# Small products between the rows of the next in-projection unit, a two-row start of two units in the ramps, and a first gate that leaves ahead of a weight split

## The chip, the cores and the metric

The kernel runs on one core of one Trainium2 chip. The metric is device time in microseconds (us) of one execution of the whole program. TensorE (PE) multiplies, VectorE (DVE), ScalarE (ACT) and GpSimd (POOL) do the element work, and SyncE (SP) issues most DMAs.

## The reference, cut to what matters

One layer of a hybrid decoder on 512 prompt tokens and 32 sample tokens (544 columns), model width 1024:

```python
x = x + 0.5*rmsnorm(swiglu(rmsnorm(x)))      # FFN1, inner width 2816
x = x + rmsnorm(mix(rmsnorm(x)))             # in-projection 1024 -> 2432, four mixers, out-projection
x = x + 0.5*rmsnorm(swiglu(rmsnorm(x)))      # FFN2, inner width 2816
```

In the mixer, group C (RWKV-7) takes seven of the 19 in-projection tiles, and needs three low-rank products and a normalised key before its scan:

```python
w_log = -softplus(-(w0 + tanh(wl) @ w2)) - 0.5       # low-rank product 1, 32 rows
a     = sigmoid(a0 + al @ a2)                        # low-rank product 2, 32 rows
g     = sigmoid(gl) @ g2                             # low-rank product 3, 64 rows
kk    = k*k_k ;  kk = kk * rsqrt(max(sum(kk*kk), 1e-24))   # sum over each head of 64
```

## The kernel before, in words

**Units.** Everything is held transposed: features on the 128 partitions, the 544 tokens as columns in two halves of 272. A unit is one 128-wide slice of a weight matrix times all 1024 input features: 8 rows (one row is a block of 128 input features, index `j`), each row three products (high part times high, high times low, low times high, which together give float32 accuracy), each in two halves, so 48 matmuls at line 315 (`product`).

**What a unit needs.** SP loads its weights into one of two raw buffers. ACT rounds them to the high part (`split_hi`, line 293), DVE subtracts to get the low part (`split_lo`, line 298), and PE waits for that in `split_ready`. Four split slots are used in turn. A unit's result lies in a pair of PSUM banks until DVE takes it out.

**Every engine works through its own list in order**, written out by hand; semaphores join the lists. A step that waits holds back everything behind it on its engine.

**The ramps** (`ramp_pe`) join FFN1 to the mixer and the mixer to FFN2. The input `x` of the next part is only coming into being: DVE and ACT make its rows one after the other (`rows_dve`: update at line 507, add at 512, low part at 522; ACT's high part at 517), first for token half 0 and then for half 1. PE takes row `j` for units 0, 1 and 2 as soon as it is there, and unit 3 later; between them it makes the sums of squares (line 375, which wait for DVE's lines 487 and 490) and spreads the roots (line 384).

**The in-projection** (`mixer_pe`, `mixer_act`, `mixer_dve`). Units 0 to 3 are the ramp; units 4 to 18 follow one by one. Before unit m PE waits for `split_ready(m)` and for `in_out`: DVE has taken out unit m-2 (for m of 6 and more; its `leave`, line 2220). DVE's list is, for each m: `split_lo(m)`, `leave(m-2)`, then the token shift of that tile (`shifted`, lines 2171 to 2175, for the seven tiles of group C) and what belongs to m: the scans of the decay (m = 7), three operations for each of two halves of `kp` and `bo` (m = 8), the keys' normalisation. ACT's list is, for each m from 6: `split_hi(m)`, and then what belongs to m. The parts of it around the change stand in this order:

```python
split_hi(5); tanh, sigmoid -> lo2                                   # m = 3
wait lora 1, 2: sigmoid -> bt (two halves, line 2078)               # m = 5
split_hi(6); wait lora 3, 4: sigmoid -> bh (line 2082)              # m = 6
split_hi(7); wait lora 5, 6: copy -> gg (2086); 2 squares -> kt (2089)  # m = 7
split_hi(8); wait kk_max: root (line 2092)                          # m = 8
split_hi(9); exponentials of the decay, half 0 (2097 to 2103)       # m = 9
split_hi(10); exponentials, half 1                                  # m = 10
```

The small products of group C stand on PE in blocks between units: low-rank product 1, 2 and 3 (`lora`, line 1953) after units 4, 5 and 6; the keys' sums (line 1962) after unit 7; the spread of their roots (line 2054) after unit 8; the bonus' sums (line 1974) after unit 10. These products are plain float32, and one of them shows as two matmul instructions. ACT reads the two halves of `lora` with one step each, and the next low-rank product waits for that step (`lora_out`), since it writes to the same banks. POOL starts the pooling mixer's additions (lines 1368 to 1374) once DVE has taken out unit 8.

**The start of an FFN.** Units are gate and up in turn: unit 0 is the gate of inner tile 0, unit 1 its up, units 2 and 3 those of tile 1. DVE multiplies the gate by the norm (line 1105, semaphore `gate`), ACT applies silu (line 1095), DVE multiplies by the up (line 1109, `h_mul`) and splits the result (`hidden_dve`). In the loop over the other tiles (`ffn_pe`, group 0) PE waits, before each unit, for the split, and for the hidden tile that frees its banks (`h_mul`). In FFN2 ACT's list is `split_hi(4)`, silu; DVE's is `split_lo(4)`, then the whole of `hidden_dve` for tile 0, then the rows of `qb` (lines 970 and 971).

Of the kernel before, what the change touches and what calls it, by code (L numbers as in the profile page):

```python
# [30 lines left out]
P = 128  # L31
# [83 lines left out]
def program(nc, a, o):  # L115

    with ExitStack() as ctx:
# [138 lines left out]
        def pair(n):  # L256
            return ps[:, 2 * n:2 * n + 2, 0:H]
# [312 lines left out]
        def ramp_pe(pe, n, u):  # L570

            def come(h, j):
                pe.wait_ge(S("n_xl"), row(n, h, j) + 1)

            pe.wait_ge(S("n_rb"), mark(n, 0, 0) + 1)
            for j in range(KD):
                come(0, j)
                for s in range(3):
                    if j == 0:
                        split_ready(pe, u, 0, s)  # L580
                    product(pe, pair(s), s, (j,), xh, xl, opens=j == 0, closes=j == KD - 1, parts=(0,))
                if j == 2:
                    half_sums_pe(pe, n, 1, 0)
                if j == 3:
                    half_sums_pe(pe, n, 1, 1)
                    half_spread_pe(pe, n, 1, 0)
                if j == 4:
                    pe.wait_ge(S("n_rb"), mark(n, 0, 1) + 1)
                    split_ready(pe, u, 0, 3)
                    product(pe, pair(3), 3, range(5), xh, xl, closes=False, parts=(0,))  # L590
                if j > 4:
                    product(pe, pair(3), 3, (j,), xh, xl, opens=False, closes=j == KD - 1, parts=(0,))
                if j == 5:
                    half_spread_pe(pe, n, 1, 1)
            pe.wait_ge(S("n_rb"), mark(n, 1, 1) + 1)
            for j in range(KD - 2):
                come(1, j)
                for s in range(4):
                    product(pe, pair(s), s, (j,), xh, xl, opens=j == 0, closes=False, parts=(1,))
            for s in range(4):  # L600
                product(pe, pair(s), s, (KD - 2, KD - 1), xh, xl, None if s else lambda j: come(1, j), opens=False, parts=(1,)
                        ).then_inc(S("unit_done"), 1)
# [431 lines left out]
        def ffn_pe(pe, q, u0, n):  # L1034
            u, dn = u0, 0

            def input_ready(j):
                pe.wait_ge(S("n_xl"), j + 1)

            for s in range(0 if q else 4):  # L1040
                split_ready(pe, u, 0, s)
                if s == 3:
                    pe.wait_ge(S("n_rb"), 1)
                if s == 2:
                    product(pe, pair(s), s, range(KD // 2), xh, xl, closes=False)
                    spread_root_pe(pe)
                    product(pe, pair(s), s, range(KD // 2, KD), xh, xl, opens=False).then_inc(S("unit_done"), 1)
                    continue
                product(pe, pair(s), s, range(KD), xh, xl, input_ready if s == 0 else None).then_inc(S("unit_done"), 1)
                if s == 1:  # L1050
                    pe.wait_ge(S("in_con"), 48)
                    sums_pe(pe)
            for g, (f0, nf) in enumerate(GROUPS):
                if g:
                    with pe.Fori(0, nf // 2) as i:
                        for s in range(2):
                            fast_pe(pe, q, g, i, s, dn)
                else:
                    with pe.Fori(1, nf // 2) as i:
                        for s in range(4):  # L1060
                            split_ready(pe, u, i, s)
                            pe.wait_ge(S("h_mul"), i * 2 + (FT * q + f0 + s // 2 + 1))
                            pe.wait_ge(S("d_out"), 20 * q + dn + s + 1)
                            product(pe, pair(s), s, range(KD), xh, xl).then_inc(S("unit_done"), 1)
                    u += 2 * nf

                def hidden_ready(j):
                    pe.wait_ge(S("h_lo"), FT * q + f0 + j + 1 + 2)

                def down_free(d):  # L1070
                    pe.wait_ge(S("d_out"), 20 * q + dn + d + 1)

                if g == 2:
                    for s in range(4):
                        split_ready(pe, u, 0, s)
                        pe.wait_ge(S("h_mul"), FT * q + f0 + nf + 2 - (s < 2))
                        down_free(s)
                        product(pe, pair(s), s, range(nf), hh, hl, hidden_ready if s == 0 else None
                                ).then_inc(S("unit_done"), 1)
                    last_units_pe(pe, 4 * q + 1, u, 0, range(nf), hh, hl, down_free)  # L1080
                    continue
                with pe.Fori(0, 2) as i:
                    for s in range(4):
                        split_ready(pe, u, i, s)
                        pe.wait_ge(S("h_mul"), FT * q + f0 + nf + 2 - (s < 2))
                        pe.wait_ge(S("d_out"), i * 4 + (20 * q + dn + s + 1))
                        product(pe, pair(s), s, range(nf), hh, hl, hidden_ready if s == 0 else None
                                ).then_inc(S("unit_done"), 1)
                u += KD
                dn += KD  # L1090
# [4 lines left out]
            act.activation(silu[:, s % 2], silu[:, s % 2], ACT.Silu).then_inc(S("silu"), 1)  # L1095

        def hidden_dve(dve, q, u, i, f0, s):

            unit_done(dve, u, i, 2 * s)
            dve.wait_ge(S("h_mul"), i * 2 + (FT * q + f0 + s + 1))  # L1100
# [2 lines left out]
            else:  # L1103
                dve.wait_ge(S("n_rb"), 1)
            dve.tensor_tensor(halves(silu[:, s % 2]), pair(2 * (s % 2)), halves(rb[:]), MUL).then_inc(S("gate"), 1)
            unit_done(dve, u, i, 2 * s + 1)
            dve.wait_ge(S("silu"), i * 2 + (FT * q + f0 + s + 1))
            dve.wait_ge(S("h_lo"), i * 2 + (FT * q + f0 + s + 1))
# [34 lines left out]
        def ffn_act(act, q, u0, n):  # L1143
# [4 lines left out]
            for g, (f0, nf) in enumerate(GROUPS):  # L1148
# [12 lines left out]
                for s in range(0 if q == 0 else 4, 4):  # L1161
                    if s > 1:
                        split_hi(act, u, 0, s, KD)
                    if s == 3:
                        root_act(act)
                        rb_act(act)
                if q:
                    split_hi(act, u + 4, 0, 0, KD)
                silu_act(act, q, 0, f0, 0)
                for s in range(1 if q else 0, 2 * nf - 4):  # L1170
# [13 lines left out]
        def ffn_dve(dve, q, u0, n):  # L1184
# [4 lines left out]
            for g, (f0, nf) in enumerate(GROUPS):  # L1189
# [7 lines left out]
                for s in range(0 if q == 0 else 4, 4):  # L1197
                    if s > 1:
                        split_lo(dve, u, 0, s, KD)
                    if s == 3:  # L1200
                        stats_dve(dve)
                if q:
                    split_lo(dve, u + 4, 0, 0, KD)
                hidden_dve(dve, q, u, 0, f0, 0)
                if q:
                    rows_mul_dve(dve, q, 0, False)
                for s in range(1 if q else 0, 2 * nf - 4):
# [728 lines left out]
        def mixer_pe(pe):  # L1936
            A, B = pair(2), pair(3)

            ramp_pe(pe, 1, MIX0)
            for m in range(4, NIN):  # L1940
                split_ready(pe, MIX0, 0, m)
                in_out(pe, {4: 0, 5: 1}.get(m, m - 2))
                product(pe, pair(in_pair(m)), m % 4, range(KD), xh, xl).then_inc(S("unit_done"), 2 if m == NIN - 1 else 1)
                if m in (4, 5, 6):

                    rows = (slice(0, 32), slice(32, 64), slice(64, P))[m - 4]
                    in_out(pe, 3)
                    for p in range(2):
                        pe.wait_ge(S("lo2"), 1)
                        if m > 4:  # L1950
                            pe.wait_ge(S("lora_out"), 2 * (m - 4) - 1 + p)
                        for n in range(2):
                            last = pe.matmul((A, B)[p][:, n], lora_w[rows, P * p:P * p + P],
                                             (lo if m == 5 else lo2)[rows, n * H:n * H + H], start=True, stop=True)
                        last.then_inc(S("lora"), 1)
                if m == 7:
                    pe.wait_ge(S("lora_out"), 5)
                    pe.wait_ge(S("kk_sq"), 2)
                    for p in range(2):
                        for t in range(5):  # L1960
                            c = (p * 5 + t) * 2
                            last = pe.matmul(ps[:, 4, c:c + 2], kt[:, p, tok(t)], hsel, start=True, stop=True)
                    last.then_inc(S("kk_sum"), 1)
                if m == 8:
                    pe.wait_ge(S("kk_rec"), 1)
                    pe.wait_ge(S("lora_out"), 6)
                    for p in range(2):
# [89 lines left out]
        def mixer_act(act):  # L2057
            for m in range(3, NIN + 2):
# [24 lines left out]
                if m == 7:  # L2083
# [3 lines left out]
                    for p in range(2):  # L2087
                        act.wait_ge(S("kkraw"), p + 1)
                        act.activation(kt[:, p], ar[:, p, 0], ACT.Square).then_inc(S("kk_sq"), 1)
                if m == 8:  # L2090
                    act.wait_ge(S("kk_max"), 1)
                    act.activation(st[:, 1, 0:20], st[:, 0, 0:20], ACT.Sqrt).then_inc(S("kk_root"), 1)
                if m in (9, 10):
# [40 lines left out]
        def mixer_dve(dve):  # L2134
# [89 lines left out]
            for m in range(2, NIN + 2):  # L2224
# [51 lines left out]
                if m == 8:  # L2276
                    for p in range(2):
# [2 lines left out]
                        do(dve.tensor_scalar(tmp2[:, p], bh[:, p], par_("ka", p), onemka[:, p:p + 1], MUL, ADD))  # L2280
                        do(dve.tensor_tensor(kp[:, p], kp[:, p], tmp2[:, p], MUL))
                        dve.scalar_tensor_tensor(bo[:, p], ar[:, p, 1], par_("rk", p), kp[:, p], MUL, MUL).then_inc(S("rk"), 1)
                    dve.wait_ge(S("kk_sum"), 1)
                    dve.tensor_scalar(st[:, 0, 0:20], ps[:, 4, 0:20], 1e-24, None, ALU.max).then_inc(S("kk_max"), 1)
                    dve.wait_ge(S("kk_root"), 1)
# [241 lines left out]
```

## Time and profile before

| | |
|---|---|
| median of 3 runs | 1118.23 us (1114.58 to 1122.45) |
| the profiled execution | 1122.75 us, its span 1120.9 us |
| mean granted clock of PE | 0.961 |
| PE busy (weight loads) | 1073.6 us, 96% (1050.4 us, 94%) |
| DVE, ACT, POOL busy | 798.0, 461.6, 275.6 us |
| DMA | 92.04 MB, mean 82 GB/s |

Busy time of PE counts a matmul from start to its modelled end, so that matmuls overlap. "PEclk" is the granted clock: 1.00 is 2.4 GHz, 0.50 is 1.2 GHz. A timeline row gives start, duration, the instruction and, in brackets, how long the engine had been idle and what ended that. A row marked x2 or more merges instructions that follow each other. The stages in the profiled execution: FFN1 up to 391 us, the first ramp 391 to 427, the in-projection's other units 427 to 536, the rest of the mixer to 720, the second ramp 720 to 755, FFN2 to the end.

### The profile page before, as it was taken

The page shows a single profiled execution, that of the slowest core. Times are in us where ns is not written, and L with a number is a line of the kernel's source. Part 1 is how long each engine was busy: PE and PEld are TensorE (multiplying, and loading weights), DVE is VectorE, ACT ScalarE, POOL GpSimd, SP SyncE. Part 2 cuts the span into 40 slices and gives each one's busy share as a digit, 9 for nine tenths or more (in the row PEclk, how much of TensorE's full clock was granted, in tenths as well). Part 3 has the DMA queues.
Part 4 walks back from the last instruction along what each step waited for, and adds up shares of the span by engine and source line. Part 5 has one row for each costly group of instructions (what it writes and reads, how often), then busy time and mean ns, then how long its engine had stood idle before and what let it go on. Part 6 is the DMA issues. An engine that isn't in the chain of part 4 may idle for free. (4 is left out here: it accounts for less than half of the span.)

```text
span 1120.9 us, 23284 instructions
## 1 busy us (share of the span) xinstructions
PE 1073.6 (96%) x9138; PEld 1050.4 (94%) x9138; DVE 798.0 (71%) x1224; ACT 461.6 (41%) x776; POOL 275.6 (25%) x217
## 2 busy tenths in 40 slices
PE   6999999999999989999799999999999999999995
PEld 6999999999999989999677789899999999999995
DVE  5667689536986886888769627967577984399746
ACT  6423455414654433522134433433235552256520
POOL 0220656034540000120223000004125531255201
PEclk9999999999999989999779989989999999999998
DMA  6322233322324121232601002203132324223212
GB/s 215 97 90 91 84 112 108 102 91 76 112 75 132 40 71 57 79 68 87 68 2 40 2 1 80 74 23 110 58 130 75 112 75 150 76 75 112 91 60 81
DMA packets 35400, 92.04 MB, mean 82 GB/s; under 512 B 10368, under 2 KB 12928, under 8 KB 35328
## 3 DMA queue, kind: packets, MB, share of 16 engines
q1 hardware_dynamic: 34320, 88.78, 25.7%
q10 hardware_dynamic: 1008, 2.27, 0.6%
q8 instruction: 49, 0.80, 0.3%
q14 instruction: 23, 0.19, 0.1%
HBM read 87.76 MB, written 3.28 MB: 81 GB/s over the span
## 5 line engine op out<-in xcount | busy, mean ns | idle before, releaser
L315 PE MATMUL ps<-xh,wh 128*128 128x272 f32 x816 | 195.3, 302 | 18.8 <-DVE xl L499 8.6
L824 PE MATMUL ps<-seven,wh 128*128 128x272 f32 x1024 | 195.1, 287 | 0.0
L315 PE MATMUL ps<-xl,wh 128*128 128x272 f32 x816 | 191.0, 297 | 0.0
L315 PE MATMUL ps<-xh,wl 128*128 128x272 f32 x816 | 190.8, 297 | 0.0
L298 DVE TENSOR_TENSOR wl<-raw,wh 128x1024 fp32r<-128x1024 f32 (+1 forms) x99 | 118.7, 1201 | 81.1 <-ACT wh L293 80.7
L315 PEld LDWEIGHTS ps<-xh,wh 128*128 128x128 f32 x816 | 140.8, 197 | 21.9 <-DVE wl L298 12.1
L824 PEld LDWEIGHTS ps<-seven,wh 128*128 128x128 f32 x1024 | 159.8, 188 | 0.0
L315 PE MATMUL ps<-hh,wh 128*128 128x272 f32 x704 | 156.2, 288 | 0.0
L315 PE MATMUL ps<-hh,wl 128*128 128x272 f32 x704 | 155.4, 288 | 0.0
L315 PE MATMUL ps<-hl,wh 128*128 128x272 f32 x704 | 155.1, 287 | 0.0
L293 ACT ACTIVATE wh<-raw 128x1024 fp32r<-128x1024 f32 (+1 forms) x99 | 100.0, 1018 | 126.8 <-PE ps L315 58.7
L824 PE MATMUL ps<-seven,wl 128*128 128x272 f32 x512 | 146.7, 286 | 0.0
L315 PEld LDWEIGHTS ps<-xl,wh 128*128 128x128 f32 x816 | 141.4, 198 | 0.0
L315 PEld LDWEIGHTS ps<-xh,wl 128*128 128x128 f32 x816 | 140.5, 198 | 0.0
L802 DVE TENSOR_TENSOR wl<-sums,wh 128x1024 fp32r<-128x1024 f32 x64 | 93.6, 1463 | 42.2 <-ACT wh L797 42.0
L315 PEld LDWEIGHTS ps<-hl,wh 128*128 128x128 f32 x704 | 114.1, 188 | 0.0
L315 PEld LDWEIGHTS ps<-hh,wl 128*128 128x128 f32 x704 | 113.8, 188 | 0.0
L315 PEld LDWEIGHTS ps<-hh,wh 128*128 128x128 f32 x704 | 113.7, 188 | 0.0
L780 POOL TENSOR_TENSOR sums<-raw 128x512 f32<-128x512 f32 x32 | 42.6, 1331 | 282.5 <-DMA raw<-in_w_gu 246.8
L824 PE MATMUL ps<-xl,wh 128*128 128x272 f32 x384 | 111.1, 289 | 0.0
L824 PE MATMUL ps<-xh,wh 128*128 128x272 f32 x384 | 110.4, 287 | 0.0
L824 PE MATMUL ps<-xh,wl 128*128 128x272 f32 x384 | 109.9, 286 | 0.0
(348 smaller groups left out, 1910.4 us busy)
## 6 DMA issues: line engine op xcount, KB each, us to landing
raw<-in_w_gu SPq DMA_DIRECT2D x88, 512.0 KB, 3.7
raw<-in_w_d SPq DMA_DIRECT2D x32, 512.0 KB, 3.6
raw<-in_w_in SPq DMA_DIRECT2D x19, 512.0 KB, 3.6
raw<-in_w_d SPq DMA_DIRECT2D x16, 384.0 KB, 3.0
raw<-in_w_out SPq DMA_DIRECT2D x8, 512.0 KB, 3.6
out_y<-x SPq DMA_DIRECT2D x16, 136.0 KB, 1.8
x<-in_x ACTq DMA_DIRECT2D x4, 272.0 KB, 5.5
x<-in_x SPq DMA_DIRECT2D x4, 272.0 KB, 6.6
```

Of the source, the lines that this page charges most:

```text
L293: act.activation(wh[:, s % 4, 0:k, :], src[:, s % RAW, 0:k, :], ACT.Copy).then_inc(S("w_hi"), 1 + skip)
L298: dve.tensor_tensor(wl[:, s % 4, 0:k, :], src[:, s % RAW, 0:k, :], wh[:, s % 4, 0:k, :].bitcast(F32), SUB).then_inc(S("w_lo"), 1 + skip)
L315: last = pe.matmul(out[:, n], left[:, s, j], right[:, j, n * H:n * H + H], start=first and opens and j == order[0], stop=final and closes ...
L780: pool.tensor_tensor(sum_(0), up[:, 0:4], up[:, 4:8], ADD).then_inc(S("f_sum"), 1)
L802: dve.tensor_tensor(left_to(wl, k), left_of(s, k), left_to(wh, k).bitcast(F32), SUB).then_inc(S("f_lo"), 1)
L824: last = pe.matmul(out, left[:, j], right[:, j], start=m in (0, 1, 3) and j == 0 and left is hi and right is high, stop=j == 3 and left is ...
```

## The change

In the ramps, units 0 and 1 take rows 0 and 1 first, and unit 2 opens at row 1 with both rows. In the in-projection, low-rank product k (0, 1, 2) is issued inside unit 5+k, a quarter of it before each of the rows 1, 3, 5 and 7; the keys' sums are issued inside unit 8, a fifth before each of the rows 3 to 7; the spread stands after unit 9. ACT's root and DVE's three steps for it move from m = 8 to m = 9. In the FFNs' group 0, a gate unit waits for `gate` of the tile two before it (its banks have been read) and no longer for `h_mul`; in FFN2, DVE takes out the first gate before `split_lo(4)`, and ACT issues a one-column silu ahead of `split_hi(4)`. ACT's order of splits and low-rank steps stays.

```diff
@@ ramp_pe
-                for s in range(3):
-                    if j == 0:
+                for s in range(2 if j == 0 else 3):
+                    if j == s // 2:
                         split_ready(pe, u, 0, s)
-                    product(pe, pair(s), s, (j,), xh, xl, opens=j == 0, closes=j == KD - 1, parts=(0,))
+                    product(pe, pair(s), s, range(2) if j + s == 3 and j == 1 else (j,), xh, xl, opens=j == s // 2, closes=j == KD - 1,
+                            parts=(0,))
@@ ffn_pe, group 0
-                            pe.wait_ge(S("h_mul"), i * 2 + (FT * q + f0 + s // 2 + 1))
+                            if s % 2:
+                                pe.wait_ge(S("h_mul"), i * 2 + (FT * q + f0 + s // 2 + 1))
+                            else:
+                                pe.wait_ge(S("gate"), i * 2 + (FT * q + f0 + s // 2 - 1))
@@ ffn_act
                 if q:
+                    act.activation(st2[:, 1, 7:8], ones[:, 0:1], ACT.Silu)
                     split_hi(act, u + 4, 0, 0, KD)
@@ ffn_dve   (hidden_dve is cut into first_gate_dve and second_dve)
+                first_gate_dve(dve, q, u, 0, f0, 0)
                 if q:
                     split_lo(dve, u + 4, 0, 0, KD)
-                hidden_dve(dve, q, u, 0, f0, 0)
+                second_dve(dve, q, u, 0, f0, 0)
@@ mixer_pe
+            def lora_pe(k, p, n):
+                rows = (slice(0, 32), slice(32, 64), slice(64, P))[k]
+                if p + n == 0:
+                    in_out(pe, 3)
+                    pe.wait_ge(S("lo2"), 1)
+                if k and n == 0:
+                    pe.wait_ge(S("lora_out"), 2 * k - 1 + p)
+                last = pe.matmul((A, B)[p][:, n], lora_w[rows, P * p:P * p + P], (lo if k == 1 else lo2)[rows, n * H:n * H + H],
+                                 start=True, stop=True)
+                if n:
+                    last.then_inc(S("lora"), 1)
+            def keys_sum_pe(t):
...
+            def between(m):
+                def before(j):
+                    if m in (5, 6, 7) and j % 2:
+                        lora_pe(m - 5, j // 4, j // 2 % 2)
+                    if m == 8 and j > 2:
+                        keys_sum_pe(j - 3)
+                return before
...
-                product(pe, pair(in_pair(m)), m % 4, range(KD), xh, xl).then_inc(S("unit_done"), 2 if m == NIN - 1 else 1)
-                if m in (4, 5, 6):
...
-                if m == 7:
...
-                if m == 8:
+                product(pe, pair(in_pair(m)), m % 4, range(KD), xh, xl, between(m)).then_inc(S("unit_done"), 2 if m == NIN - 1 else 1)
+                if m == 9:
                     pe.wait_ge(S("kk_rec"), 1)
@@ mixer_act
-                if m == 8:
+                if m == 9:
                     act.wait_ge(S("kk_max"), 1)
@@ mixer_dve
+                if m == 9:
                     dve.wait_ge(S("kk_sum"), 1)
```

## Rows read from the trace of the kernel before

**Rows 1.** The chain that ended last, FFN2: start us, us, what.
```profile
757.08 85.66 PE ps L315 x672
926.74 47.79 PE ps L315 x384
```

**Rows 2.** Timeline of PE around units 4 to 11 of the in-projection.
```profile
433.27 0.41 PE L315 MATMUL ps<-xh,wl 128*128 128x272 f32 x2
434.45 2.07 PE L1953 MATMUL ps<-lor,lora_w 32*128 32x272 f32 x8 [0.77 <-ACT lor L2074]
436.45 0.77 PE L315 MATMUL ps<-xh,wh 128*128 128x272 f32 x2
...
444.19 2.10 PE L1953 MATMUL ps<-lor,lora_w 32*128 32x272 f32 x8
...
460.59 2.29 PE L1962 MATMUL ps<-con,kt 128*128 128x2 f32 x20
...
470.46 2.17 PE L2054 MATMUL ps<-con,st 128*64 128x128 f32 x40
...
484.70 2.00 PE L1974 MATMUL ps<-bo,con 128*128 128x272 f32 x8
```

**Rows 3.** Timeline of ACT in the in-projection.
```profile
436.55 0.72 ACT L2078 ACTIVATE bt<-ps,par 128x544 f32<-128x544 f32 x1 [0.20 <-PE ps L1953]
437.17 1.05 ACT L293 ACTIVATE wh<-raw 128x1024 fp32r<-128x1024 f32 x1
...
455.09 1.20 ACT L2089 ACTIVATE kt<-ar 128x544 f32<-128x544 f32 x2
...
466.68 1.28 ACT L2097 ACT_TABLE_LOAD   x1
467.98 0.21 ACT L2097 ACTIVATE pend<-ll 128x8 f32<-128x8 f32 x1
```

**Rows 4.** Timeline of DVE in the in-projection.
```profile
438.25 1.23 DVE L298 TENSOR_TENSOR wl<-raw,wh 128x1024 fp32r<-128x1024 f32 x1
439.39 0.85 DVE L2220 TENSOR_TENSOR pc<-ps,rb 128x272 f32<-128x272 f32 x3
...
457.26 1.22 DVE L298 TENSOR_TENSOR wl<-raw,wh 128x1024 fp32r<-128x1024 f32 x1
...
465.30 0.17 DVE L2284 TENSOR_SCALAR st<-ps 128x20 f32<-128x20 f32 x1
...
474.33 2.38 DVE L2293 SCALAR_TENSOR_TENSOR bhkh<-ar,bhkh 128x544 f32<-128x544 f32 x1
...
479.63 2.21 DVE L298 TENSOR_TENSOR wl<-raw,wh 128x1024 fp32r<-128x1024 f32 x1
```

**Rows 5.** Three stretches: busy of PE, PEld, DVE, ACT, POOL, PEclk, DMA share, GB/s.
```profile
433.50:441.00 7.50, 6.74 (x34) 5.96 (x33) 7.36 (x18) 3.17 (x5) 0.00 (x0) 0.77 0.06 11
462.00:470.00 8.00, 8.00 (x54) 8.00 (x55) 5.63 (x11) 4.44 (x9) 0.00 (x0) 0.79 0.12 29
757.00:761.00 4.00, 3.92 (x19) 3.92 (x20) 3.93 (x7) 0.16 (x1) 1.26 (x1) 0.57 0.23 90
```

**Rows 6.** The first ramp: PE opens unit 2; then DVE's low part of row 2.
```profile
394.54 0.39 PE L315 MATMUL ps<-xh,wh 128*128 128x272 f32 x1 [2.06 <-DVE wl L298]
395.70 0.50 DVE L522 SCALAR_TENSOR_TENSOR xl<-x,par,xh 128x272 fp32r<-128x272 f32 x1
```

**Rows 7.** The start of FFN2: timelines of ACT, DVE and PE.
```profile
752.57 1.06 ACT L293 ACTIVATE wh<-raw 128x1024 fp32r<-128x1024 f32 x1 [3.44 <-PE ps L315]
753.65 1.28 ACT L1095 ACT_TABLE_LOAD   x1
753.66 1.23 DVE L298 TENSOR_TENSOR wl<-raw,wh 128x1024 fp32r<-128x1024 f32 x1 [4.00 <-ACT wh L293]
754.81 0.72 DVE L1105 TENSOR_TENSOR silu<-ps,rb 128x544 f32<-128x544 f32 x1
757.08 0.59 PE L315 MATMUL ps<-xh,wh 128*128 128x272 f32 x2 [2.35 <-DVE h L1109]
```

More of the change, by code:

```diff
@@ L1097, in hidden_dve, with first_gate_dve @@
         def hidden_dve(dve, q, u, i, f0, s):
+            first_gate_dve(dve, q, u, i, f0, s)
+            second_dve(dve, q, u, i, f0, s)
+        def first_gate_dve(dve, q, u, i, f0, s):
             unit_done(dve, u, i, 2 * s)
@@ L1105, in hidden_dve, with second_dve @@
             dve.tensor_tensor(halves(silu[:, s % 2]), pair(2 * (s % 2)), halves(rb[:]), MUL).then_inc(S("gate"), 1)
+        def second_dve(dve, q, u, i, f0, s):
             unit_done(dve, u, i, 2 * s + 1)
@@ L1937, in mixer_pe @@
             A, B = pair(2), pair(3)
+            def lora_pe(k, p, n):
[10 more added lines that the diff above has]
+            def keys_sum_pe(t):
+                if t == 0:
+                    pe.wait_ge(S("lora_out"), 5)
+                    pe.wait_ge(S("kk_sq"), 2)
+                for p in range(2):
+                    c = (p * 5 + t) * 2
+                    last = pe.matmul(ps[:, 4, c:c + 2], kt[:, p, tok(t)], hsel, start=True, stop=True)
+                if t == 4:
+                    last.then_inc(S("kk_sum"), 1)
+            def between(m):
[5 more added lines that the diff above has]
+                return before
             ramp_pe(pe, 1, MIX0)
@@ L1942, in mixer_pe @@
                 in_out(pe, {4: 0, 5: 1}.get(m, m - 2))
-                product(pe, pair(in_pair(m)), m % 4, range(KD), xh, xl).then_inc(S("unit_done"), 2 if m == NIN - 1 else 1)
-                if m in (4, 5, 6):
[L1946 to L1955, printed above, removed]
-                if m == 7:
[L1957 to L1963, printed above, removed]
-                if m == 8:
+                product(pe, pair(in_pair(m)), m % 4, range(KD), xh, xl, between(m)).then_inc(S("unit_done"), 2 if m == NIN - 1 else 1)
+                if m == 9:
                     pe.wait_ge(S("kk_rec"), 1)
```

## The prediction, made before the changed kernel was run

> **What bounds the kernel now.** I read the chain of waits first. In FFN2 it is PE's own stream of full-size products [rows 1]: one matmul per 47.79/384 = 0.1245 us, so a unit of 48 takes 6.0 us and a row of one unit 0.75 us. PE is the bound there, and what is won or lost ahead of FFN2 reaches the end whole. I then read PE's timeline through the stretches that the change touches, and looked for its gaps and for the small products. In the in-projection PE hardly stops: one gap of 0.77 us before the first low-rank block, and then blocks of 2.1, 2.3, 2.2 and 2.0 us [rows 2]. So an order that hides these blocks' waits can win little, and one that opens a new gap loses it. Last I read ACT and DVE between the same times, to see what stands between a low-rank product and the next unit's weights: ACT's `bt` step ends, and `split_hi(6)` starts at once [rows 3]. That is the order of ACT's list, not of its data.
>
> The granted clock is the second thing to see. The 7.5 us after the gap of 0.77 ran at 0.77, the 8 us after the keys' block at 0.79, and the 4 us after FFN2's opening gap of 2.35 at 0.57 [rows 5, 7]: each time a spell at 1.2 GHz instead of 2.4, at the price of 7.5 x 0.23, 8 x 0.21 and 4 x 0.43, that is 1.7 us of PE's time each.
>
> **Low-rank products inside units.** The matmuls are the same and cost the same 2.1 us a block wherever they stand [rows 2]. What changes is when their last part comes. Unit 5 can start at 433.5, right behind unit 4 [rows 2], 2.9 us before its 436.45, and saves the gap and the spell after it. It then holds the first low-rank product, 6.0 + 2.1 = 8.1 us, the last quarter in front of row 7. ACT can't finish `bt` before that quarter is out, and `split_hi(6)` is behind `bt`. From the start of the second `bt` step to `split_hi(6)` is 437.17 - 436.55 = 0.6 us, from there to `split_lo(6)` 1.1 us, from there to the taking out of unit 4, which unit 6 also needs, 1.1 us, and that takes 0.85 us [rows 3, 4]: 3.7 us with hand-overs. Row 7 covers 0.75 us of it. PE stands still for 3.0 us before unit 6, where it had the low-rank block of 2.1 us to work on before. Unit 7 is behind `bh`, inside unit 6, in the same way: 3.0 us. Unit 8 is behind `gg` and ACT's two squares, 1.1 us more [rows 3]: 4.1 us. (The next low-rank product waits for `lora_out` of the last, long given.)
>
> Starts, at full clock: unit 5 at 433.5, unit 6 at 433.5 + 8.1 + 3.0 = 444.6, unit 7 at 455.7, unit 8 at 455.7 + 8.1 + 4.1 = 467.9, unit 9 at 467.9 + 6.0 + 2.3 = 476.2, and behind it the spread, so unit 10 at 476.2 + 6.0 + 2.2 = 484.4. Before, unit 10 started 6.0 ahead of the bonus block, at 478.7 [rows 2]. That is **+5.7 us**, with the two spells of before (in units 5 and 8) on the old side and none on the new.
>
> What could be late next: DVE's own work from `split_lo(8)` to the keys' maximum is 465.30 - 457.26 = 8.0 us [rows 4], and with `split_lo(9)` and a taking out it now runs from 2.0 us before unit 8 to 8.0 us after its start; unit 8 ends 8.3 after it. I cost it at nothing; without that cover it would be tenths. The keys' steps moved to m = 9 end before unit 9's sixth us, and DVE's and ACT's parts of 0.2 to 0.3 us lie beside unit 9: nothing. Behind the root on ACT come a table load, half a set of exponentials and `split_hi(10)`; they have unit 9 and the spread, 8.2 us, as cover: nothing. The row shows the load at 1.28 us with the next step 0.02 us behind it [rows 3]. By the Trainium skill (ScalarE: Activation LUTs, What ACT_TABLE_LOAD costs) a switch costs a drain of about 1.38 us more; by that ACT would be later by as much at each load, and unit 10 by a few tenths. I take the row. After the spread DVE now starts on the keys only about when unit 10 does. From 474.33 to 479.63 and `split_lo(11)` of 2.21, both long because POOL's additions run beside them [rows 4], and a taking out, make some 9 us from the spread's middle; unit 10 and the bonus block are 8.0. POOL's work is released by the same unit, so it runs beside the same DVE steps as before. I take nothing, and 1 us as the upper bound. SP's loads of weights follow `split_lo` two units earlier, and move with it.
>
> **The clock.** Gaps of 3.0, 3.0 and 4.1 us are each longer than the 0.77, 2.06 and 2.35 us after which PE's clock fell or PE waited [rows 2, 6, 7]. I take one spell after each: 3 x 1.7 = **+5.1 us**. Below, nothing; above, two spells for each, 10.2 us. The keys' sums, spread over five rows, should save their spell, which the +5.7 has already counted.
>
> **Ramps.** In the first ramp PE waited 2.06 us for unit 2's split and restarted at 394.54. Row 1 for units 0 and 1, 0.75 us, now goes into that gap, and unit 2's two rows end at about 395.3. But row 2's low part leaves DVE at 395.70 + 0.50 = 396.2 [rows 6], and DVE waits for nothing that moved. So PE stops there instead: **0**, with 0.6 us as the bound on either side (what a shifted gap could do to the clock). The second ramp has the same order: 0.
>
> **The start of FFN2.** PE waited 2.35 us for DVE's line 1109 [rows 7]. Now the first gate leaves while ACT makes `split_hi(4)`; DVE's split still ends at 753.66 + 1.23 = 754.9, and that is what unit 4 waits for, since its banks are free once the gate (0.72 us, from 752.5) is out. It starts at about 754.95 instead of 757.08: 2.1 us, and the spell behind the gap, 1.7 us, goes too, since 0.4 us of gap is under all that were followed by one. **-3.8 us.** ACT's new one-column silu and the table load of 1.28 us fall in its idle 3.44 us before 752.57 [rows 7]. Unit 5's split follows 1.5 us earlier, ahead of its need. Bounds: 0 and -3.8. In the other loops DVE has finished a hidden tile before the split that PE also waits for: nothing.
>
> **Sum.** 5.7 + 5.1 + 0 - 3.8 = +7.0 us on the profiled execution, 1122.75 + 7.0 = 1129.8. That execution is 4.5 us above the median of the runs, so I put the forecast at 1118.23 + 7.0 = **1125.2 us**. About 1%, 11.2 us, is what a measurement can tell from no change.
>
> **Rivals.**
> - *Slower by over 1%.* In units 6, 7 and 8 each gap costs two spells at 1.2 GHz. It decides once a gap is so long that the clock does not come back after one spell; for it speaks that the gaps are longer than any seen before in these stretches, against it that 2.35 us cost just one [rows 5, 7]. 5.7 + 10.2 - 3.8 = +12.1: 1130.3 us. Chance 0.22.
> - *The gaps come, the clock holds.* 5.7 - 3.8 = +1.9: 1120.1 us. Against it speak the rows of the three spells. Chance 0.08. The Trainium skill (TensorE: Matmul & The Clock Gate, HAM oscillation) lets the clock fall back only over long waits between bursts; by that this rival would be the likely one, and the trace here does not agree, with its spell after 2.35 us.
> - *The splits are not held up*, because ACT comes to them earlier than I read from its list. Then PE saves the gap and the spells of units 5 and 8, 0.8 + 3.4, and FFN2's 3.8: 1110.2 us. Against it: the split starts as `bt` ends [rows 3]. Chance 0.07.
> - *FFN2's gain does not come*, something else holding unit 4: +10.8, 1129.0 us. Chance 0.06.
> - The forecast, one spell for each gap: chance 0.57, its own range 1121 to 1130.
>
> **Range and chances.** From between the third rival's time and the second's up to past the first's, with the 4 us by which runs scatter: 1115 to 1133. Slower by over 1% (above 1129.4): the first rival's most, and the upper tail of the forecast and of the fourth, 0.22. Faster by over 1% (below 1107): a part of the third, 0.03. Within: 0.75.
>
> **What would show it.** Right: PE's timeline has gaps near 3 us in front of units 6 and 7 and near 4 in front of unit 8, each ended by DVE (split or taking out), with ACT's `split_hi` right behind `bt`, `bh` and the squares; PEclk below 1 after each; no block of low-rank products between units; unit 4 of FFN2 starting behind DVE's line 298 with under 1 us of gap. Wrong: these gaps missing or under 1 us, ACT's splits ahead of its low-rank steps, or a total under 1115 us.

## The result: slower by 2.0%, where +0.6% was forecast

| | forecast | measured |
|---|---|---|
| median | 1125.2 us (1115 to 1133) | 1142.47 us (1137.88 to 1143.73, 4 runs) |
| the kernel before, beside it | | 1120.34 us (1114.58 to 1125.5, 4 runs) |
| ratio | 1.006 | 1.0198 [1.0154, 1.0241] |
| profiled execution, its span | 1129.8 us | 1142.94 us, 1141.2 us |
| mean granted clock | | 0.955 (before 0.961) |

The direction is right and the size is not: the time lies 9 us above the range. The first rival, slower by over 1% through a second spell at 1.2 GHz behind each gap, had 0.22; its own time, 1130.3 us, is too low as well. The experiments below were timed in three sets, each on another chip, with the kernel before beside them (its medians: 1123.01, 1122.21 and 1121.03 us); so results of different sets are compared by their ratios to it, with their 95% intervals, and the ratio is not the quotient of the two medians.

The page of the changed kernel shows PE's busy time and the granted clock in 40 slices of 28.5 us. Slices 16 and 17 (428 to 485 us) hold the changed units of the in-projection, and their digits are 8 and 7.

```profile
span 1141.2 us, 23289 instructions
PE 1084.3 (95%) x9138; PEld 1054.5 (92%) x9138; DVE 799.4 (70%) x1224; ACT 461.5 (40%) x777; POOL 276.6 (24%) x217
PEclk9999999999999988799868988989999999999998
```

PE's waits of the changed kernel (engine line, what it waited for, us in total, times, longest) hold a line that has no counterpart before, the first one here: three waits for the taking out of an in-projection unit, at the new number 2245 of line 2220. The second, a wait of the scan for its start states, was 2.0 us before.

```profile
PE ps L315 <- DVE pc L2245: 9.7, 3, 3.9
PE ps L1743 <- DMA s0t<-in_s: 4.7, 1, 4.7
```

PE's timeline of the changed kernel shows them ([rows 2] is the same stretch before). The columns are start, duration of the group, and in brackets the idle time before it with what ended it.

```profile
425.87 0.52 PE L315 MATMUL ps<-xh,wh 128*128 128x272 f32 x2 [0.22 <-DVE wl L298]
...
434.89 0.41 PE L315 MATMUL ps<-xh,wl 128*128 128x272 f32 x2
435.23 0.72 PE L1959 MATMUL ps<-lor,lora_w 32*128 32x272 f32 x2
435.88 0.52 PE L315 MATMUL ps<-xh,wh 128*128 128x272 f32 x2
...
437.58 0.72 PE L1959 MATMUL ps<-lor,lora_w 32*128 32x272 f32 x2
...
439.94 0.72 PE L1959 MATMUL ps<-lor,lora_w 32*128 32x272 f32 x2
...
444.52 0.60 PE L315 MATMUL ps<-xh,wh 128*128 128x272 f32 x2 [2.91 <-DVE pc L2245]
...
445.96 1.27 PE L1959 MATMUL ps<-lor,lora_w 32*128 32x272 f32 x2
...
450.19 1.27 PE L1959 MATMUL ps<-lor,lora_w 32*128 32x272 f32 x2
...
461.62 0.63 PE L315 MATMUL ps<-xh,wh 128*128 128x272 f32 x2 [2.92 <-DVE pc L2245]
...
479.71 0.79 PE L315 MATMUL ps<-xh,wh 128*128 128x272 f32 x2 [3.91 <-DVE pc L2245]
...
496.85 2.17 PE L2079 MATMUL ps<-con,st 128*64 128x128 f32 x40
...
505.07 2.00 PE L1999 MATMUL ps<-bo,con 128*128 128x272 f32 x8
```

The gaps stand before units 6, 7 and 8, with 2.91, 2.92 and 3.91 us. Two more things are in these rows. From one quarter of a low-rank product to the next, two rows of the unit lie between, and it takes 437.58 - 435.23 = 2.35 us; two rows are 1.50 us, so a quarter costs 0.85 us, not 2.1/4 = 0.53. And in unit 6 the same piece takes 450.19 - 445.96 = 4.23 us, at half the clock (its granted clock is in the stretches below).

ACT's timeline of the changed kernel shows what the gaps wait for, as [rows 3] let foresee it: each split starts as the second low-rank step ends, and for unit 8 behind the squares.

```profile
440.69 0.72 ACT L2103 ACTIVATE bt<-ps,par 128x544 f32<-128x544 f32 x1 [3.99 <-PE ps L1959]
441.31 1.05 ACT L293 ACTIVATE wh<-raw 128x1024 fp32r<-128x1024 f32 x1
...
457.79 0.72 ACT L2107 ACTIVATE bhkh<-ps,par 128x544 f32<-128x544 f32 x1 [5.58 <-PE ps L1959]
458.40 1.05 ACT L293 ACTIVATE wh<-raw 128x1024 fp32r<-128x1024 f32 x1
...
474.88 0.62 ACT L2111 ACTIVATE gg<-ps 128x544 f32<-128x544 f32 x1 [5.65 <-PE ps L1959]
475.40 1.19 ACT L2114 ACTIVATE kt<-ar 128x544 f32<-128x544 f32 x2
476.50 1.99 ACT L293 ACTIVATE wh<-raw 128x1024 fp32r<-128x1024 f32 x2
```

Now the profile by stretches, from one unit's start to the next (stretch, its length, then busy time of PE, PEld, DVE, ACT and POOL with their instructions, the granted clock, DMA share, GB/s): units 4 and 5 with the gap behind them, units 6 and 7 with theirs, and units 8 and 9 with part of the spread. Behind them stand the three spells at 1.2 GHz by themselves.

```profile
425.87:444.50 18.63, 15.72 (x104) 13.44 (x105) 12.74 (x33) 5.90 (x7) 0.00 (x0) 1.00 0.19 56
444.50:461.60 17.10, 14.18 (x56) 10.91 (x57) 3.71 (x9) 2.38 (x3) 0.00 (x0) 0.70 0.10 32
461.60:479.70 18.10, 14.18 (x56) 10.93 (x57) 8.96 (x17) 5.42 (x7) 0.07 (x1) 0.69 0.09 29
479.70:498.90 19.20, 19.19 (x156) 19.05 (x156) 10.84 (x22) 8.60 (x17) 3.01 (x6) 0.84 0.25 69
...
444.50:454.90 10.40, 10.38 (x35) 8.24 (x36) 1.63 (x4) 0.72 (x1) 0.00 (x0) 0.51 0.16 52
461.80:472.00 10.20, 10.20 (x35) 8.04 (x35) 6.67 (x12) 0.62 (x1) 0.00 (x0) 0.50 0.15 49
478.90:485.70 6.80, 5.99 (x27) 6.02 (x28) 6.48 (x14) 0.89 (x1) 1.72 (x5) 0.50 0.27 80
```

Unit 6 with its pieces is PE-busy for 14.18 us, where a unit is 6.0 and its four quarters are 3.4 at full clock. From unit 4's start to the bonus block the changed kernel takes 505.07 - 425.87 = 79.2 us; before it was 484.70 - 427.40 = 57.3 (the block is in [rows 2], the start is this row of PE's timeline before). That is +21.9 us, more than the whole loss.

```profile
427.40 0.52 PE L315 MATMUL ps<-xh,wh 128*128 128x272 f32 x2 [0.22 <-DVE wl L298]
```

In FFN2 the forecast order has come: the gate, the split, and unit 4 behind DVE's line 298 ([rows 7] before). First ACT, DVE and PE of the changed kernel there, then its chain of waits through FFN2 (start, us, what), which answers to the first row of [rows 1].

```profile
772.18 1.28 ACT L1179 ACT_TABLE_LOAD   x1
775.55 0.73 DVE L1113 TENSOR_TENSOR silu<-ps,rb 128x544 f32<-128x544 f32 x1 [2.85 <-PE ps L315]
776.70 1.23 DVE L298 TENSOR_TENSOR wl<-raw,wh 128x1024 fp32r<-128x1024 f32 x1 [0.42 <-ACT wh L293]
778.17 0.49 PE L315 MATMUL ps<-xh,wh 128*128 128x272 f32 x2 [0.40 <-DVE wl L298]
```

```profile
778.17 84.19 PE ps L315 x672
```

The gap is 0.40 us instead of 2.35, and the 672 matmuls take 84.19 us instead of 85.66.

### The profile page after: what moved, and what is told of

The parts are those of the page before. It is cut to its first block, busy times and chain, and to the rows that moved or that the text cites. A ratio compares the mean times of both kernels' runs of the same rounds, so it can differ in the third digit from the quotient of the medians.

```text
span 1141.2 us, 23289 instructions
## 1 busy us (share of the span) xinstructions
PE 1084.3 (95%) x9138; PEld 1054.5 (92%) x9138; DVE 799.4 (70%) x1224; ACT 461.5 (40%) x777; POOL 276.6 (24%) x217
## 4 chain that ended last, share of the span: by engine, by line
PE 85%; DVE 9%; DMA 2%; ACT 2%; issue 2%; SPq 0%; ACTq 0%; DVEq 0%
PE ps L315 46%; PE ps L825 29%; DMA s0t<-in_s 1%; DVE mixf L1334 1%; DVE wl L298 1%; PE ps L375 1%; PE ps L1959 1%; PE ps L1515 1%; PE ps L1508 1%; PE ps L1517 1%; ACT wh L293 1%; PE ps L384 1%; DMA x<-in_x 1%; DVE tb L684 1%; PE ps L1743 0%
```

## The experiments

Theory at the start: the gaps and the lower clock behind them, both out of the in-projection's order, make the loss. Rival: another part does (ramps or FFN2), or the pieces inside units cost by themselves.

**In-projection alone.** The kernel before with only the edits of `mixer_pe`, `mixer_act` and `mixer_dve`:

```diff
+                product(pe, pair(in_pair(m)), m % 4, range(KD), xh, xl, between(m))...
-                if m in (4, 5, 6):            # the three blocks between units
+                        lora_pe(m - 5, j // 4, j // 2 % 2)   # in between(m)
```

> The kernel before with the in-projection's part of the change alone (low-rank products and keys' sums inside units, spread after unit 9); ramps and FFN2 as before. Theory 1, the loss is all there: ratio to the kernel before 1.020 to 1.024 (22 to 26 us more), since the whole change gained 2 to 4 us elsewhere. Rival, a part of the loss lies in the ramps or in FFN2: ratio 1.015 or less.

Measured: 1138.48 us (1134.19 to 1144.54, 4 runs), ratio 1.015 [1.0093, 1.0206], with gaps of 2.91, 2.92 and 3.92 us. Most of the loss is here, but the ratio is the rival's bound and lies below the 1.020 to 1.024 that the theory expected; the interval holds both. The run is repeated below.

**FFN2 alone.** The kernel before with only the first gate ahead of the split, ACT's one-column silu and the wait for `gate` in the loop. The main part of it:

```diff
+                first_gate_dve(dve, q, u, 0, f0, 0)
                 if q:
                     split_lo(dve, u + 4, 0, 0, KD)
-                hidden_dve(dve, q, u, 0, f0, 0)
+                second_dve(dve, q, u, 0, f0, 0)
```

> The kernel before with FFN2's first gate ahead of the split and the gate wait in the loop, nothing else. Theory 1: unit 4 of FFN2 starts about 0.4 us behind the ramp instead of 2.35, with no spell at 1.2 GHz behind it: 3.7 us less, ratio 0.9967. Rival: the gain is taken back in the loop (another wait before units 5 to 7): ratio 1.000.

Measured: 1121.35 us (12 runs), 0.9968 [0.9935, 1.0]; gap 0.40 us and no spell behind it. By the ratio that is a gain of about 3.6 us, and the interval's end touches none (the two medians are 1.7 us apart).

**Splits first.** The changed kernel, with ACT's splits for units 6 to 8 ahead of its low-rank steps; PE's order stays. This takes the suspected cause away alone:

```diff
+                if m in (5, 6, 7):
+                    split_hi(act, MIX0, 0, m + 1, KD)
-                if m >= 6:
+                if m >= 9:
                     split_hi(act, MIX0, 0, m if m < NIN else m + 1, ...)
```

> The changed kernel with one edit in ACT's list: the high splits of units 6, 7 and 8 stand ahead of the low-rank steps bt, bh and gg instead of behind them. Theory 1 (the held split opens the gaps, and the clock falls because of the gaps): no gap before units 6, 7, 8, granted clock 1.00 in units 5 to 8, and what remains is the cost of the quarters, 0.85 us each instead of 0.53: the kernel is 20 to 25 us faster than the changed one and about 4 us faster than the kernel before, ratio 0.994 to 0.999. Rival A (the 32- and 64-row products themselves take the clock down once they are spread over the units): gaps gone, but spells of 5 to 10 us at 1.2 GHz in units 6 and 7, ratio 1.003 to 1.010. Rival B (something else on ACT or DVE holds the units): gaps of 2 us and more remain, ratio over 1.01.

Measured: 1122.93 us (10 runs), 1.0013 [0.9982, 1.0044]. ACT's timeline of this kernel has the split ahead of `bt`, and its stretch from unit 4 on has no gap and the full clock:

```profile
434.47 1.06 ACT L293 ACTIVATE wh<-raw 128x1024 fp32r<-128x1024 f32 x1
437.67 0.72 ACT L2105 ACTIVATE bt<-ps,par 128x544 f32<-128x544 f32 x1 [2.15 <-PE ps L1959]
```

```profile
427.50:486.00 58.50, 58.44 (x427) 51.92 (x428) 43.87 (x87) 23.54 (x34) 10.54 (x9) 1.00 0.27 67
```

PE is busy 58.44 of 58.50 us. Two lines moved on ACT give back nearly all of the loss: the ratio falls from 1.0198 to 1.0013, the medians from 1142.47 to 1122.93 us. Yet the in-projection is hardly faster than before, though it has neither gap nor spell: unit 4 to bonus block is 484.48 - 427.54 = 56.9 us, before 57.3. The dearer quarters eat what is won there. The expected 0.994 to 0.999 had FFN2's gain in it as well and was missed; where that gain went in this kernel is not accounted for.

**Block before row 7.** The changed kernel, each low-rank product as one block ahead of the last row of its unit:

```diff
-                    if m in (5, 6, 7) and j % 2:
-                        lora_pe(m - 5, j // 4, j // 2 % 2)
+                    if m in (5, 6, 7) and j == 7:
+                        for i in range(4):
+                            lora_pe(m - 5, i // 2, i % 2)
```

> The changed kernel with each low-rank product as one block of four in front of row 7 of units 5, 6 and 7, instead of a quarter before each of the rows 1, 3, 5, 7. The last part stands where it stood, so the gaps of 2.9, 2.9 and 3.9 us stay. Theory 1 (the small products keep the clock low once a gap has brought it down): the spells behind the gaps in units 6 and 7 are shorter, 3 to 7 us instead of the changed kernel's 10, and each unit saves 1.0 us of switching between kinds of products: 6 to 10 us faster than the changed kernel, ratio to before 1.010 to 1.014. Rival (the gap's length alone sets the spell): spells of 10 us, ratio 1.016 to 1.018.

Measured: 1134.69 us (4 runs), 1.0106 [1.0057, 1.0154], gaps 2.92, 2.92 and 3.90 us. The gaps stay and the products are cheap again. The three spells are 6.8 us long each and cost 3.4 us each, 10.2 in all; but 2.7 of these fall into the ends of the gaps, where PE stands still anyhow, so its work loses 7.6.

**Ramps alone.** The kernel before with only the two-row start:

```diff
-                for s in range(3):
+                for s in range(2 if j == 0 else 3):
```

> The kernel before with the two-row start of units 0 and 1 in both ramps, nothing else. Theory (DVE paces the ramps; PE only stops at another place): ratio 1.000, within 0.998 to 1.002. Rival A (the stops that the new order makes, 0.7 and 1.3 us close together, keep the clock at 1.2 GHz longer, as the second ramp of the changed kernel shows with 10.2 us where the kernel before had 7.0): 1.7 to 5 us more, ratio 1.0015 to 1.005. Rival B (the wait filled by row 1 shortens the ramps): ratio 0.998 or less.

Measured: 1119.27 us (12 runs), 0.998 [0.9956, 1.0004]. No loss; a gain of 2 us is not told from none. This run shows something else: FFN2's gap of 2.35 us is still there, and the clock holds behind it, where [rows 5] has 0.57 for the same stretch before.

```profile
754.10:758.10 4.00, 3.99 (x32) 3.99 (x32) 3.97 (x6) 0.09 (x1) 1.33 (x1) 1.00 0.19 75
```

**The changed kernel once more.** No edit:

> The changed kernel again, unchanged, for a second profile and more runs of its time. Theory 1 (the gaps of 2.9, 2.9 and 3.9 us are fixed by the order of ACT's list; the length of the spells behind them varies from run to run): the three gaps within 0.05 us of the first profile's, the spells in units 6, 7 and 8 anywhere from 3.4 to 10.2 us each, ratio 1.013 to 1.022. Rival (the spells are fixed as well): 10.2, 10.2 and 6.8 us again, ratio 1.019 to 1.021.

Measured: 1139.27 us (1137.08 to 1143.21, 4 runs), 1.0166 [1.012, 1.0212]. Its gaps are the same, 2.92, 2.92 and 3.92 us; its spells are not. Its units 6 and 7:

```profile
446.00:464.60 18.60, 15.68 (x56) 11.89 (x57) 3.69 (x9) 2.37 (x3) 0.00 (x0) 0.61 0.10 29
464.60:480.90 16.30, 12.37 (x57) 9.62 (x57) 8.99 (x17) 5.46 (x7) 0.10 (x1) 0.81 0.11 32
```

Unit 6 takes 15.68 us of PE and unit 7 12.37, where both took 14.18 in the first execution of the same program. The length of a spell varies between two executions of one program. Behind the first gap it was 13.7 us, longer than the 3.4 to 10.2 expected. So the order of the instructions alone does not set it.

**Full rows.** The changed kernel with the quarters taken over all 128 rows instead of 32 or 64. This replaces the low-rank products by others, so that the kernel's output is no longer that of the reference; the order of work is the same:

```diff
-                last = pe.matmul((A, B)[p][:, n], lora_w[rows, ...], (lo if k == 1 else lo2)[rows, ...], ...)
+                last = pe.matmul((A, B)[p][:, n], lora_w[:, ...], lo[:, ...], ...)
```

> The changed kernel with its low-rank quarters taken over all 128 rows of the operands instead of 32, 32 and 64 rows (the product is another one, of the same number of columns and matmuls). Same places, same gaps. Theory 1 (products of few rows keep the clock low after a gap): the spells behind the gaps of units 6 and 7 fall to 7 us or less, 3 to 7 us faster than the changed kernel in the same job. Rival (rows don't matter to the clock; the gap and its timing set the spell): the same time as the changed kernel within 2 us, and the 0.85 us for a quarter stays too, which would show that the switch between kinds of product and not the row count makes a quarter dear.

Measured: 1129.74 us (7 runs), 1.0085 [1.0052, 1.0118], 9.5 us less than the changed kernel beside it. PE's timeline of this kernel in unit 5, then its weight loads there:

```profile
436.46 0.62 PE L1959 MATMUL ps<-lor,lora_w 128*128 128x272 f32 x2
...
438.43 0.62 PE L1959 MATMUL ps<-lor,lora_w 128*128 128x272 f32 x2
```

```profile
436.34 0.31 PEld L1959 LDWEIGHTS ps<-lor,lora_w 128*128 128x128 f32 x2
436.69 0.42 PEld L315 LDWEIGHTS ps<-xh,wh 128*128 128x128 f32 x2
```

The weight loads of the changed kernel at the first quarter:

```profile
432.88 0.29 PEld L1959 LDWEIGHTS ps<-lor,lora_w 32*128 32x128 f32 x2 [0.21 <-issue]
433.53 0.30 PEld L315 LDWEIGHTS ps<-xh,wh 128*128 128x128 f32 x2 [0.36 <-issue]
```

With 32 rows the weight loads are idle for 0.21 us ahead of the quarter's and for 0.36 us behind them, and the quarter costs 0.85 us; with 128 rows there is no such idle time and the spacing is 1.97, the quarter 0.47 us, although it has four times the rows. So the dearer quarter is the price of the switch between a few-row product and full ones. The Trainium skill (TensorE: Matmul & The Clock Gate, Step-by-step: what each phase is for) says that PE pulls a weight load ahead of running matmuls where the row groups don't conflict or the load goes to the background weight buffer. The two timelines fit a pull-ahead that is lost next to 32-row products. They do not show why, and no run here separates this from another cost of the switch.

The three gaps are 3.12, 3.12 and 4.11 us here. 12 quarters at 0.38 less give 4.6 of the 9.5 us; the other 5 come with shorter spells (6.8 us lost in the profiled execution, 13.7 and 11.9 in those of the changed kernel). That the rows shortened the spells is not shown: the in-projection alone, with its few-row quarters, lost 6.8 us as well.

**Block before row 1.** If a block is cheap and the split must not wait, the block belongs at the front of the unit. The kernel before with the FFN2 part and the in-projection part, but each low-rank product as one block ahead of row 1 (as in the edit above, `j == 1`); ramps as before:

> The kernel before with the FFN2 part, the keys' sums inside unit 8 with the spread after unit 9, and each low-rank product as one block of four in front of row 1 of units 5, 6 and 7; the ramps as before. The low-rank results then come before row 1, so ACT's list holds no split. Theory 1: no gap before units 5 to 8, no spell in them, and no more switching than before: the in-projection gains 0.8 us of gap and 3.4 us of spells, FFN2 3.7 us: 8 us less, ratio 0.990 to 0.995. Rival (blocks inside a unit cost as the quarters do, or the clock falls in them): ratio 0.997 to 1.000.

Measured: **1113.02 us** (12 runs), 0.9942 [0.9915, 0.9969]: faster than the changed kernel, and 0.6% faster than the one before. PE's timeline of this kernel, ACT's, and the stretch from unit 4 on:

```profile
434.47 2.07 PE L1958 MATMUL ps<-lor,lora_w 32*128 32x272 f32 x8
...
442.67 2.10 PE L1958 MATMUL ps<-lor,lora_w 32*128 32x272 f32 x8
...
480.88 2.00 PE L1999 MATMUL ps<-bo,con 128*128 128x272 f32 x8
```

```profile
436.58 0.71 ACT L2103 ACTIVATE bt<-ps,par 128x544 f32<-128x544 f32 x1 [0.20 <-PE ps L1958]
437.19 1.05 ACT L293 ACTIVATE wh<-raw 128x1024 fp32r<-128x1024 f32 x1
```

```profile
427.40:482.80 55.40, 55.35 (x429) 52.52 (x430) 44.27 (x87) 23.41 (x34) 10.95 (x9) 1.00 0.28 70
```

The split still stands right behind `bt` on ACT, but seven rows of unit 5 (5.25 us) are left to cover it. Row 0 covers the 0.77 us in which PE waited for `lo2` before. Unit 4 to bonus block is 480.88 - 427.42 = 53.5 us, 3.8 less than before. From block to block are 442.67 - 434.47 = 8.20 us; less the eight rows between (6.0) that is 2.2 for a block, 0.56 us for each of its four products, by the same measure by which a quarter costs 0.85.

**The same with the ramps' part:**

> The kernel of e8 with the ramps' part of the change added, so the changed kernel with each low-rank product as one block in front of row 1. If the ramps cost nothing in the whole either: 0.992 to 0.996 against the kernel before, as e8's 0.9942. Rival (in the whole kernel the new ramp order costs 2 to 5 us of clock in the second ramp, which would explain why the changed kernel is not faster than the in-projection part alone): 0.996 to 1.000.

Measured: 1117.82 us (12 runs), 0.998 [0.9959, 1.0001]. Alone the ramps' part gave -2 us, here it gives +4, and the ratio's interval overlaps that of the kernel above. The two profiled executions are 3.9 us apart (spans 1114.3 and 1110.4). 1.7 of it is in the second ramp, which loses 6.8 us to the clock where the kernel above loses 5.1; 2.1 lie ahead of it, where the ramps' part changes nothing and the wait for the scan's start states was 2.6 us instead of 0.9. What the part does stays open.

**In-projection alone, once more,** with six runs:

> The in-projection's part of the change alone once more, with more rounds, since its 1.015 (1.009 to 1.021) lies below what the whole change minus FFN2's gain gives. If the parts add up: 1.018 to 1.024. Rival (they don't, and the FFN2 or ramp part costs something beside the in-projection's): 1.012 to 1.016.

Measured: 1140.25 us (6 runs), 1.019 [1.015, 1.023], beside 1.0198 and 1.0166 for the whole change. So the in-projection's part alone makes all of the loss within the intervals. Its profiled execution lost 6.8 us to the clock in units 6 to 8, as the first one did; it was one of the short ones (1136.31 us, where three of the six took 1144 to 1145).

**Quarters, splits first, ramps as before:** the kernel with the block before row 1, its blocks again cut into quarters and ACT's splits moved ahead.

> The kernel of e8 with quarters before rows 1, 3, 5 and 7 in place of blocks, and the high splits of units 6 to 8 ahead of the low-rank steps on ACT; ramps as before. Against e8 it differs by nothing but 9 more switches between kinds of product, at (0.85 - 0.53) = 0.32 us for each of 12 quarters: 3.8 us slower than e8, ratio to before 0.997 to 0.999. Rival (quarters also bring spells at 1.2 GHz without any gap): 1.000 and more.

Measured: 1120.43 us (12 runs), 1.0003 [0.9983, 1.0023], where 0.997 to 0.999 was expected. It has no gap and no spell in the in-projection. It is slower than the blocks before row 1 by 0.6% in the ratio, and by 7.4 us in the profiled executions (spans 1117.8 and 1110.4). Unit 4 to bonus block is 484.50 - 427.56 = 56.9 us against 53.5, so the quarters cost 3.5 us, as 12 x (0.85 - 0.56) says. Another 3.8 us lie between the bonus block and the second ramp, where both kernels have the same work, with one wait that differs (first this kernel, then the one with the blocks):

```profile
555.30 5.44 PE L1742 MATMUL ps<-ar,s0t 64*64 64x8 f32 x61 [4.70 <-DMA s0t<-in_s]
...
549.82 1.38 PE L1742 MATMUL ps<-ar,s0t 64*64 64x8 f32 x25 [0.95 <-DMA s0t<-in_s]
```

The scan's start states arrive by a DMA, and the wait for it was between 0.5 and 5.4 us over all profiled executions; in the two of the changed kernel, one program, it was 4.7 and 0.5. So it varies by itself, and differences of 4 us between single executions can come from it.

## Why the prediction was wrong, step by step

The forecast for the profiled execution was +7.0 us; it came to 1142.94 - 1122.75 = +20.2. The in-projection was to give 5.7 + 5.1 = +10.8 and gave +21.9.

- **The gaps: right.** 3.0, 3.0 and 4.1 us were forecast from ACT's and DVE's durations, 2.91, 2.92 and 3.91 came, behind DVE's taking out, with the split right behind `bt`, `bh` and the squares. Splits first shows the cause: without the wait in ACT's list the gaps are gone, and the loss with them (ratio 1.0198 to 1.0013).
- **The clock, +5.1: the term that failed most.** It was one short spell a gap. The three spells of the changed kernel run from 444.7 to 454.9, 461.8 to 472.0 and 478.9 to 485.7, and take 5.1, 5.1 and 3.4 us, of which 0.4 lies in the last gap: 13.2 us, 8.1 more than forecast. Not even the first rival's 10.2 us holds it. The step that failed is "one spell after each: 3 x 1.7": the price was taken from single spells behind gaps of 0.77 and 2.35 us and behind the keys' block [rows 5, 7], and nothing in these rows said that it holds for a gap of 3 or 4 us. The few-row quarters in units 6 and 7 were a suspect. Full rows (6.8 us lost) and the whole block ahead of row 7 (10.2, of which PE's work felt 7.6) point that way; against it, the in-projection alone, with the same quarters, also lost only 6.8 us twice, and the changed kernel itself lost 13.7 and 11.9 in two executions. So the loss behind a gap of 2.9 us is known to vary between 1.7 and 6.8 us; what sets it stays open. Whether it is the moment at which the gap falls was not tested.
- **Quarters at the block's price: wrong.** "The matmuls are the same and cost the same 2.1 us a block wherever they stand" was the step. A quarter costs 0.85 instead of 0.53 us: 12 x 0.32 = +3.9 us (0.4 of it because a block takes 2.2 us by this measure and not 2.1). 8.1 + 3.9, less 0.4 for the gaps, are 11.6, against the 11.1 us that the in-projection went beyond its forecast; 0.5 is what this count is off by.
- **What could be late next: right.** The keys' chain, the table loads and the spread of the roots cost nothing: no idle time of PE stands before the spread at 496.85 or the bonus block at 505.07.
- **Ramps, 0: roughly right.** In the first ramp PE stopped at another place, as forecast: its wait for unit 2's split fell from 2.06 to 1.30 us, and new stops followed. From the end of that wait to unit 4 it took 425.87 - 392.97 = 32.9 us, before 427.40 - 394.54 = 32.9. The second ramp with FFN2's start went from 757.08 - 719.87 = 37.2 us (from the spread's row in PE's timeline) to 778.17 - 741.98 = 36.2. FFN2's gap gave 1.95 of it, so the ramp cost 0.9; timed alone, the ramps' part cost nothing.
- **FFN2, -3.8: right in order, in size nearly.** Gap -1.95 (forecast 2.1), spell 85.66 - 84.19 = -1.5 (1.7). The ramps' run weakens the reason for the spell: the same gap of 2.35 us, full clock behind it.
- **Not foreseen:** a longer wait for the scan's start states, 4.7 us instead of 2.0, in a stretch from the bonus block to the second ramp's spread that took 1.7 us more; the wait varies by itself, as the changed kernel's second profile shows. Against it unit 4 started 1.5 us earlier than before, and PE was as much earlier already when it opened unit 2 in the first ramp: the profiled execution before has a spell of 3.4 us at 1.2 GHz about 27 us after its start, the two of the changed kernel have none there, the one with full rows has it again. So neither belongs to the change.

The sum, forecast 7.0: +11.1 in-projection, -1.5 earlier start, +1.7 middle, +1.3 ramp and FFN2, +0.6 behind it: 20.2, as measured.

The table load of 1.28 us has the next step 0.02 us behind it in the changed kernel too, so the row was the right choice over the drain that the forecast named.

## What to carry to other kernels

Small products hide inside a large unit only if their consumer's step is not ahead of the next unit's preparation in an in-order list: move them to the unit's front, or move the preparation ahead. Keep few-row products together, since every switch to full-size ones costs PE about 0.3 us. Price a new gap of about 3 us on PE at its length plus what the clock takes behind it, and give that a range: it was 2 to 7 us here. And before a difference of 4 us between two single executions is explained, look for the waits and spells that also differ between two executions of one program.

## What the runs showed of the hardware that was not expected

- A 32-row product of 272 columns in float32 between full-size ones costs 0.85 us, the same product with 128 rows 0.47 us, and a 32-row one in a block of four 0.56 us (2.1/4 = 0.53 by the duration that the timeline shows). The weight load behind the first is idle for 0.36 us.
- Gaps of 2.9 to 3.1 us were followed, in six profiled executions, by losses to the clock between 1.7 and 6.8 us each; FFN2's gap of 2.35 us was followed by a spell in three executions and by none in one.
